# Key tile first in the opening, scalings on GpSimd, and another timetable for the attention steps of a decoder layer on eight cores

## The chip, the cores and the metric

One program runs on the 8 NeuronCores of one Trainium2 chip. Each core has a TensorE (PE), a VectorE (DVE), a ScalarE (ACT), a GpSimd (POOL), a SyncE (SP) that issues transfers, and 16 DMA engines. The metric is device time of the slowest core, in microseconds (us). The cores exchange nothing; each takes one of four sequences and one half of it.

## The reference

A decoder layer over `x` (4 x 4096 x 1024, float32) with a conditioning vector `c` per sequence. Cut to what matters here:

```python
mod = silu(c) @ w_ada + b_ada                      # (B, 6D): sh1, sc1, gt1, sh2, sc2, gt2
h   = rmsnorm(x, g_norm_mix) * (1 + sc1) + sh1
proj = h @ w_in + b_in                             # xin, bg, cg, q, k, v, o, gates, gate_c, gate_m
y_conv = bg * causal_dwconv(cg * xin, conv_mix_w)
hm  = mlstm_chunkwise(q, k, v, ig, fg)             # 128 tokens a chunk, a 128 x 256 state per head
z   = sigmoid(gate_c) * (y_conv @ w_proj_conv) + sigmoid(gate_m) * ((sigmoid(o) * headnorm(hm)) @ w_proj_mlstm)
x   = x + gt1 * (z @ w_out)
h   = rmsnorm(x, g_norm_ffn) * (1 + sc2) + sh2
a, g = split(h @ w_up)
x   = x + gt2 * ((silu(causal_dwconv(a)) * g) @ w_down)
out = rmsnorm(x, g_final)
```

The mLSTM carries a state through all 4096 tokens, so the core with the second half of a sequence needs the state that the first half leaves.

## The kernel before

**The prefix.** Each core first takes 2048 tokens (16 tiles of 128, the last one of 124) that stand before its own half. Of them it needs only the state: keys and gates for each tile, and one matrix. A tile n is loaded into a buffer of `xt` (10 buffers, queue of SP, `ask_x`), its sum of squares and root are made on ACT (L433, L436), the reciprocal and the scaling to bf16 on DVE (L442, L453), into `xnp[n]`. Four such tiles make a group. `tgroup` transposes a group on PE (32 matmuls against the identity, L484), and eight evacuations multiply by the gain `G1 = (1 + sc1) * g` and add the shift `sh1`: four on ACT (L488), four on DVE (L492). `kproj(c)` then makes the keys of a tile in 8 matmuls of 512 columns (L691), a DVE add of the bias (L693), and 8 small gate matmuls (L626).

**The opening's order.** POOL issues the weight transfers, which convert float32 to bf16, in the order in which they are first used: two tiles of `w_ada` for the scale (`ada_cols(2)`, `ada_cols(3)`), two for the shift (0 and 1), then the key tile of `w_in`; at most five are issued ahead until `allow_w` waits for an x tile and lifts the limit. Four x tiles are asked for at once, the next only when the third weight tile has landed. `ada_cols` is 32 matmuls of one column (L403). After the prefix come nine "front" tiles (the core's own first 4 + 1024 tokens), transposed in three groups into `hT`, then the gate matmuls of `stage_gates` and the projection of q, between whose four heads the steps of `gates_prefix` stand. Last comes the prefix state: 144 matmuls of 512 columns (L1348), which need every key tile scaled by the gate weights (L1337).

**The stages.** The core's own 2048 tokens are worked in two stages of 1024: projections (k, v, o), then a stretch in which the convolution branch's projections (x, c, b; `proj_blocks`, L508) run on PE while the mLSTM's chunk steps are put in between, then the merge, the output projection, and the FFN (up and down). Stage 0 has 9 chunks and blocks of 512, 258 and 258 columns, and 8 further blocks for modulation tiles (`unit_ada`); stage 1 has 8 chunks and blocks of 512.

**The table of the chunk steps.** `parts` (L1019) gives each step of chunk c a position in units of a chunk; position times `per` blocks says after how many projection blocks it is issued. The steps: `at_K` transposes the keys (PE L826, DVE L828), `at_A` makes the scores (PE L838, DVE L841 four times), `at_X` the outputs (PE L856 and L858 into banks 4 to 7, one ACT copy L860 of all four banks), `at_new` the new state (PE L867 into banks 4 to 7, DVE L869 four times), `at_old` the scaled bf16 state (ACT L847), `at_den`, `at_sq`, `at_f`, `at_hm` the head norm (DVE and ACT), `at_D` transposes back (PE L913, DVE L915 twice). During this stretch banks 4 to 7 are reserved for `at_X` and `at_new`; `at_K`, `at_A`, `at_D` and the projections take turns on banks 0 to 3 (`next_bank`). Every engine executes its own instructions in order.

**The down projection.** During the down projection of stage 0 (L1258), `during_down` loads, normalises (DVE L453) and transposes (PE L484) the x tiles of stage 1, one tile per output chunk; each tile's transfer is asked for in the same job that uses it.

## Time and profile before

| | us |
|---|---|
| median of 3 runs (lowest, highest) | 1375.95 (1372.84, 1376.09) |
| the profiled execution's own time | 1372.99 |
| its span on core 4, the slowest | 1371.7 |
| spans of the 8 cores | 1362.9 to 1371.7 |
| PE busy (share of the span) | 1263.1 (92%) |
| DVE, ACT, POOL busy | 697.5 (51%), 529.2 (39%), 76.5 (6%) |
| chain that ended last, PE's share | 83% |

All times below are microseconds from the start of the span on core 4. PEclk is the granted TensorE clock as a share of 2.4 GHz, 0.5 being 1.2 GHz. Idle time of an engine is named with what ended it ("<- DVE arena L453"). `arena` is one large buffer that holds most tiles, so a line number says more than its name.

### The profile page before, as it was taken

To read this page: it belongs to the slowest core of one execution; us is meant where nothing else is said; L and a number is where in the kernel's file an instruction comes from. 1 tells how busy PE (TensorE), PEld (TensorE's weight loads), DVE (VectorE), ACT (ScalarE), POOL (GpSimd) and SP (SyncE) were. 2 spreads that over 40 slices of the span, in tenths; PEclk is the share of its full clock that TensorE was granted. 3 is DMA by queue.
4 is the path that set the end of the run, shared out by engine and by line. 5 is a ranking of instruction groups with operands and counts; after the bars stand their busy time and mean duration, and the time that the engine had idled before them with its cause. 6 is when DMAs were issued, how large, how long until landed. Compare 5 with 4: busy or idle time off the path is not lost.

```text
span 1371.7 us, 21457 instructions; the slowest of 8 cores (1362.9 to 1371.7 us)
## 1 busy us (share of the span) xinstructions
PE 1263.1 (92%) x7662; PEld 690.8 (50%) x7662; DVE 697.5 (51%) x1268; ACT 529.2 (39%) x1013; POOL 76.5 (6%) x149
## 2 busy tenths in 40 slices
PE   0677999997899999999998999989999999999998
PEld 0354455665656665666654444444444444444443
DVE  0574332576843346555654423378732365556534
ACT  2464122654522225544433331465522245544202
POOL 1000000000000000000000000000000000100000
PEclk9997999999999999999999999999999999999999
DMA  9988024267493646343252782505346074441503
GB/s 174 233 194 136 1 39 75 50 107 124 85 189 60 106 91 131 69 81 63 46 111 85 175 154 54 101 1 93 84 101 112 13 152 93 74 81 32 108 0 123
DMA packets 35128, 130.38 MB, mean 95 GB/s; under 512 B 2764, under 2 KB 3020, under 8 KB 35024
## 3 DMA queue, kind: packets, MB, share of 16 engines
q0 software_dynamic: 24944, 93.74, 40.6%
q1 hardware_dynamic: 10080, 35.27, 7.8%
q8 instruction: 64, 1.05, 0.3%
q14 instruction: 40, 0.33, 0.1%
HBM read 214.34 MB, written 8.39 MB: 162 GB/s over the span
## 4 chain that ended last, share of the span: by engine, by line
PE 83%; DVE 6%; DMA 4%; ACT 3%; issue 3%; POOL 0%; DVEq 0%; ACTq 0%; SPq 0%; POOLq 0%
PE psum L508 54%; PE psum L1258 11%; PE psum L1113 4%; PE psum L793 4%; DMA wslot<-w_in 3%; PE psum L1348 2%; PE psum L691 2%; PE psum L484 1%; DVE C L869 1%; DVE arena L841 1%; ACT arena L860 1%; PE psum L867 1%; DMA arena<-bada_row 1%; ACT sqj L433 1%; PE psum L418 1%
## 5 line engine op out<-in xcount | busy, mean ns | idle before, releaser
L508 PE MATMUL psum<-arena,wslot 128*128 128x512 bf16 (+1 forms) x4640 | 830.7, 339 | 11.6 <-DVE arena L915 3.8
L508 PEld LDWEIGHTS psum<-arena,wslot 128*128 128x128 bf16 x4640 | 452.5, 98 | 372.0 <-issue 31.6
L1187 DVE SCALAR_TENSOR_TENSOR arena<-arena,pcol_t 128x1028 f32<-128x1028 f32 (+1 forms) x88 | 113.3, 1287 | 92.8 <-ACT arena L1184 88.2
L1258 PE MATMUL psum<-wslot,arena 128*128 128x512 bf16 x704 | 153.2, 380 | 1.5 <-ACT arena L488 1.5
L1258 PEld LDWEIGHTS psum<-wslot,arena 128*128 128x128 bf16 x704 | 68.8, 98 | 84.2 <-issue 2.2
L1069 ACT ACTIVATE arena<-psum,pcol_t 128x512 bf16<-128x512 f32 (+1 forms) x80 | 47.9, 603 | 162.2 <-PE psum L508 161.1
L433 ACT ACTIVATE sqj<-arena 128x1024 bf16<-128x1024 f32 (+1 forms) x49 | 51.6, 1054 | 137.6 <-DVE arena L1261 96.0
L1189 ACT ACTIVATE arena<-arena 128x1028 f32<-128x1028 f32 (+1 forms) x44 | 46.6, 1059 | 121.1 <-DVE arena L1187 121.1
L1073 DVE TENSOR_TENSOR arena<-psum,arena 128x512 f32<-128x512 f32 (+1 forms) x40 | 23.3, 585 | 73.4 <-PE psum L508 72.5
L1113 PE MATMUL psum<-wslot,arena 128*128 128x512 bf16 (+1 forms) x272 | 60.3, 379 | 0.2 <-DVE arena L492 0.2
L793 PE MATMUL psum<-wslot,arena 128*128 128x512 bf16 (+1 forms) x272 | 59.2, 379 | 0.0
L488 ACT ACTIVATE arena<-psum,modc,G 128x384 bf16<-128x384 f32 (+4 forms) x64 | 39.3, 670 | 50.3 <-PE psum L484 24.2
L1195 DVE TENSOR_TENSOR arena<-psum,arena 128x512 bf16<-128x512 f32 (+1 forms) x110 | 57.8, 575 | 0.0
L1077 DVE TENSOR_TENSOR arena<-psum,arena 128x512 bf16<-128x512 f32 (+1 forms) x40 | 23.3, 583 | 67.9 <-PE psum L508 67.9
L1172 ACT ACTIVATE arena<-psum 128x512 f32<-128x512 f32 (+1 forms) x110 | 51.8, 504 | 15.0 <-PE psum L508 14.0
L887 ACT ACTIVATE sqj<-arena,sml 128x256 bf16<-128x256 f32 (+1 forms) x68 | 33.7, 497 | 59.1 <-DVE sml L881 55.0
L126 POOL DMA_DIRECT2D wslot<-w_in x32 | 22.7, 710 | 601.7 <-PE psum L508 266.3
L1184 ACT ACTIVATE arena<-arena,pcol_t 128x1028 f32<-128x1028 f32 (+1 forms) x44 | 50.6, 1150 | 14.5 <-DVE arena L1178 11.4
L1261 DVE TENSOR_TENSOR arena<-psum,arena 128x512 f32<-128x512 f32 x32 | 22.1, 692 | 66.3 <-PE psum L1258 66.3
L796 DVE TENSOR_TENSOR arena<-psum,bvbc 128x512 bf16<-128x512 f32 (+1 forms) x34 | 23.6, 694 | 42.2 <-PE psum L793 42.2
L403 PE MATMUL psum<-scol,wslot 128*128 128x1 bf16 x256 | 7.7, 164 | 40.4 <-DMA wslot<-w_ada 38.5
L492 DVE TENSOR_SCALAR arena<-psum,G,modc 128x384 bf16<-128x384 f32 (+4 forms) x64 | 39.9, 671 | 6.8 <-PE psum L484 6.6
(176 smaller groups left out, 1084.8 us busy)
## 6 DMA issues: line engine op xcount, KB each, us to landing
wslot<-w_in POOLq DMA_DIRECT2D x32, 1024.0 KB, 12.2
arena<-xin SPq DMA_DIRECT2D x32, 512.0 KB, 16.1
wslot<-w_ada POOLq DMA_DIRECT2D x12, 1024.0 KB, 13.3
wslot<-w_up_a POOLq DMA_DIRECT2D x10, 1024.0 KB, 10.1
wslot<-w_up_g POOLq DMA_DIRECT2D x10, 1024.0 KB, 11.8
wslot<-w_down POOLq DMA_DIRECT2D x8, 1024.0 KB, 9.0
y<-arena SPq DMA_DIRECT2D x16, 512.0 KB, 2.7
xt<-xin SPq DMA_DIRECT2D x15, 512.0 KB, 5.2
```

Source lines behind the costliest of these rows:

```text
L433: S.op("act", lambda e: e.activation(out=sqj[0:p, :], in_=src, func=AF.Square, accum_out=ssq[0:p]), reads=r_src, writes=[r_sqj, r_ssq])
L492: S.op("dve", lambda e: e.tensor_scalar(out=dst[:, k, col0:col0 + n], in0=psum[:, b, 0:n], scalar1=G[:, k:k + 1], scalar2=modc[:, sh0 + k: ...
L508: S.op("pe", lambda e: e.matmul(psum[:, b, 0:n], lhsT=wv[:, k, wcol0:wcol0 + 128], rhs=src[:, k, t0:t0 + n], start=(k == 0), stop=(k == 7) ...
L793: S.op("pe", lambda e: e.matmul(psum[0:p, b, :], lhsT=hT[:, k, t0:t0 + p], rhs=wslot[si_v[half]][:, k, :], start=(k == 0), stop=(k == 7)), ...
L1069: S.op("act", lambda e: e.activation(out=sg[:, t0:t0 + n], in_=psum[:, b, 0:n], func=AF.Sigmoid, bias=pcol[:, PC_B + col:PC_B + col + 1]), ...
L1113: S.op("pe", lambda e: e.matmul(psum[0:p, b, :], lhsT=zT[:, k, t0:t0 + p], rhs=wslot[si_w[i]][:, k, :], start=(k == 0), stop=(k == 7)), re ...
L1172: S.op("act", lambda e: e.activation(out=a_s[:, 2 + t0:2 + t0 + n], in_=psum[:, b, 0:n], func=AF.Copy), reads=[r_bank[b]], writes=[r_a])
L1184: S.op("act", lambda e: e.activation(out=t3[:, T0:NT], in_=a_s[:, 2 + T0:2 + NT], func=AF.Identity, scale=pcol[:, cw + 2:cw + 3]), reads=[ ...
L1187: S.op("dve", lambda e: e.scalar_tensor_tensor(out=t3[:, T0:NT], in0=a_s[:, s_ + T0:s_ + NT], scalar=pcol[:, cw + s_:cw + s_ + 1], in1=t3[ ...
L1189: S.op("act", lambda e: e.activation(out=t3[:, T0:NT], in_=t3[:, T0:NT], func=AF.Silu), reads=[r_t], writes=[r_t])
L1195: S.op("dve", lambda e: e.tensor_tensor(out=act_t[j][:, t0:t0 + n], in0=psum[:, b, 0:n], in1=t3[:, t0:t0 + n], op=ALU.mult), reads=[r_bank ...
L1258: S.op("pe", lambda e: e.matmul(psum[:, b, :], lhsT=act_t[jj][:, t0:t0 + 128], rhs=wv[:, jj % 8, :], start=(jj == 0), stop=(jj == NFF - 1) ...
```

## The change

1. **Order of the opening.** The weight order becomes scale tiles, key tile, shift tiles. x tiles 4 to 7 are asked for when the key tile has landed (`sp_after(2)`), the rest when the second shift tile has (`sp_after(4)`). Groups 0 and 1 of the prefix are evacuated with the gain alone (`transp_plain`); keys 0 to 5 leave PSUM without a bias. `ada_cols(0)` and `ada_cols(1)` come behind `kproj(3)`. The shift's contribution to keys and gates is one row, made as 16 + 16 matmuls behind `kproj(5)` from a high and a low bf16 half of the shift broadcast over 128 columns, and added later: to keys 0 to 5 by three DVE adds behind `kproj(8)` to `kproj(10)`, to keys 6 and 7 in their evacuation, to the gates at the end.
2. **Scalings on GpSimd.** For the 16 prefix and 9 front tiles the multiplication by the reciprocal root runs on POOL. The norms are issued further ahead (`norm_upto`), with four more buffers (`xfr`) for front tiles. Evacuations of transposes in the opening go to ACT every fourth time, no longer every second.
3. **gates_prefix** gets two heads of the key projection of stage 0 as further cover.
4. **Chunk steps.** `at_K` is evacuated by four ACT instructions instead of one on DVE and uses bank 6, `at_A` bank 7, `at_D` banks 4 and 5. `at_new`, `at_old` and `at_D` are split in halves; the table of positions is another one.
5. **during_down** asks for each x tile one job ahead.

```diff
@@ opening
+        S.dma("pool", bkbc, brow_d[:, 0:512].partition_broadcast(128), writes=[r_bk])
         if plan is not None:
             pump_w()
-        S.dma("pool", bkbc, brow_d[:, 0:512].partition_broadcast(128), writes=[r_bk])
...
-            norm_to(xt[i][0:p, :], [r_xt[i]], dst[0:p, :], r_dst, p)
+            src = xt[i][0:p, :]
+            sd, r_sd = rms_root(src, [r_xt[i]], p)
+            rs, r_rs = recip(sd, r_sd, p)
+            S.op("pool", lambda e: e.tensor_scalar(out=dst[0:p, :], in0=src, scalar1=rs, scalar2=None, op0=ALU.mult),
+                 reads=[r_xt[i], r_rs], writes=[r_dst])
...
         ask_x(4)
-        ada_cols(2)
-        ada_cols(3)
-        ada_cols(0)
-        ask_x()
-        for c in range(4):
-            xprefix(c)
-        ada_cols(1)
+        sp_after(2)
+        ask_x(8)
+        sp_after(4)
+        ask_x()
+        norm_upto(4)
+        tiles0 = [(xnp[c], r_xnp[c], 128) for c in range(4)]
+        banks0 = [transp_mm(tiles0, k) for k in range(6)]
+        ada_cols(2)
+        ada_cols(3)
         gain(G1, r_G1, 8, PC_GMIX)
+        for k in range(6):
+            transp_plain(tiles0, hTp[0], r_hTp[0], k, banks0[k])
...
+        NB = 6
+        for c in range(NPF):
+            norm_upto((5, 6, 7, 8, 9, 10, 11, 12, 14, 16, 18, 20, 21, 22, 23, 24)[c])
+            if c == 9:
+                allow_w(6, r_xt[xbuf[15]])
+            if c == 3:
+                tiles1 = [(xnp[i], r_xnp[i], 128) for i in range(4, 8)]
+                for k in range(8):
+                    transp_plain(tiles1, hTp[1], r_hTp[1], k, transp_mm(tiles1, k))
+            if c in (7, 11):
+                tgroup(c // 4 + 1)
+            kproj(c)
+            if c == 3:
+                ada_cols(0)
+                ada_cols(1)
...
+            if c == NB - 1:
...
+                    S.op("pe", lambda e: e.matmul(psum[:, b, :], lhsT=shbc[:, i, :], rhs=wslot[si_k][:, i % 8, :], start=(i == 0), stop=(i == 15)),
...
@@ gates_prefix
-        interleave(gates_prefix(NPF), [(lambda h=h: proj(si_q, h * 128, hT, rd_h, tbs0, evq(h))) for h in range(4)])
+        interleave(gates_prefix(NPF), [(lambda h=h: proj(si_q, h * 128, hT, rd_h, tbs0, evq(h))) for h in range(4)]
+                   + [(lambda h=h: proj(si_k, h * 128, hT, rd_h, tbs0, evk(h))) for h in range(2)])
@@ chunk steps
-            parts = [(-0.7, at_K), (-0.7, at_A), (0.2, at_X), (0.3, at_new), (0.3, at_den), (0.45, lambda c: at_sq(c, lo)), (0.55, lambda c: at_sq(c, hi)),
-                     (0.65, at_f), (0.75, lambda c: at_hm(c, lo)), (0.85, lambda c: at_hm(c, hi)), (1.45, at_D)]
-            per = nblk / (nch + 0.6)
+            parts = [(-0.42, at_K), (-0.52, at_A), (0.05, at_X), (0.22, lambda c: at_new(c, lo)), (0.22, at_den), (0.3, lambda c: at_new(c, hi)),
+                     (0.35, lambda c: at_sq(c, lo)), (0.45, lambda c: at_sq(c, hi)), (0.6, at_f), (0.7, lambda c: at_hm(c, lo)), (0.8, lambda c: at_hm(c, hi)),
+                     (1.45, lambda c: at_D(c, (0,))), (1.53, lambda c: at_D(c, (1,)))]
+            per = nblk / (nch + 0.65)
+            todo = [((c + 0.2 + f) * per, i, fn, c) for c in range(nch) for i, (f, fn) in enumerate(parts)]
...
@@ during_down
+                        if c + 1 < len(chunks):
+                            asked.append(load_x(chunks[c + 1][2], chunks[c + 1][1]))
```

Where the order moves, it is shown engine by engine. PE's queue in the opening, from the first key projections on, before (L691 is a key projection, L484 a transpose, L403 a modulation tile):

```order
2 L691 MATMUL psum<-wslot,arena 128x512 x8
3 L626 MATMUL psum<-wgate,arena 128x8 x8
4 L691 MATMUL psum<-wslot,arena 128x512 x8
5 L626 MATMUL psum<-wgate,arena 128x8 x8
6 L691 MATMUL psum<-wslot,arena 128x512 x8
7 L626 MATMUL psum<-wgate,arena 128x8 x8
8 L484 MATMUL psum<-identb,arena 128x128 x32
9 L691 MATMUL psum<-wslot,arena 128x512 x8
```

and now (L739 is the key projection, L488 the transpose, L409 a modulation tile, L775 and L778 the shift's row):

```order
7 L739 MATMUL psum<-wslot,arena 128x512 x8
8 L647 MATMUL psum<-wgate,arena 128x8 x8
9 L488 MATMUL psum<-identb,arena 128x128 x32
10 L739 MATMUL psum<-wslot,arena 128x512 x8
11 L647 MATMUL psum<-wgate,arena 128x8 x8
12 L409 MATMUL psum<-scol,wslot 128x1 x64
13 L739 MATMUL psum<-wslot,arena 128x512 x8
14 L647 MATMUL psum<-wgate,arena 128x8 x8
15 L739 MATMUL psum<-wslot,arena 128x512 x8
16 L647 MATMUL psum<-wgate,arena 128x8 x8
17 L775 MATMUL psum<-wslot,arena 128x512 x16
18 L778 MATMUL psum<-wgate,arena 128x8 x16
```

The transposes of group 1 stand ahead of the fourth key projection, as they did; two modulation tiles and the shift's row now stand behind them.

POOL's queue in the opening now, from the scaling of x tile 14 on (`d_sp10` is the semaphore of the transfer of x tile 21, `s_dve` the reciprocal):

```order
30 L681 TENSOR_SCALAR arena<-arena,stat 128x1024 [waits d_sp3,s_dve]
31 L681 TENSOR_SCALAR arena<-arena,stat 124x1024 [waits d_sp4,s_dve]
32 L126 DMA wslot5<-w_in 128x2x2048 [waits d_sp10]
33 L681 TENSOR_SCALAR xnb0<-xt0,stat 4x1024 [waits d_sp5,s_dve]
34 L681 TENSOR_SCALAR xnb1<-xt1,stat 128x1024 [waits d_sp6,s_dve]
35 L681 TENSOR_SCALAR xnb2<-arena,stat 128x1024 [waits d_sp7,s_dve]
```

Before, this queue held only transfers here; now the scalings of the nine front tiles stand behind a transfer that waits for x tile 21.

PE's queue in the chunk steps of stage 1, the third chunk before (L826 `at_K`, L838 `at_A`, L867 `at_new`, L913 `at_D`, L508 projection blocks, 8 matmuls each):

```order
555 L858 MATMUL psum<-Cb,arena 128x257
556 L826 MATMUL psum<-identb,arena 128x128 x4
557 L838 MATMUL psum<-arena 128x128 x4
558 L867 MATMUL psum<-arena 128x257 x4
559 L508 MATMUL psum<-arena,wslot 128x512 x8
560 L913 MATMUL psum<-identb,xnb 128x128 x8
561 L508 MATMUL psum<-arena,wslot 128x512 x32
```

and now (L900 `at_K`, L911 `at_A`, L938 `at_new`, L984 `at_D`, L529 projection blocks):

```order
613 L929 MATMUL psum<-Cb,arena 128x257
614 L529 MATMUL psum<-arena,wslot 128x512 x8
615 L938 MATMUL psum<-arena 128x257 x4
616 L529 MATMUL psum<-arena,wslot 128x512 x8
617 L984 MATMUL psum<-identb,xnb 128x128 x4
618 L911 MATMUL psum<-arena 128x128 x4
619 L529 MATMUL psum<-arena,wslot 128x512 x8
620 L984 MATMUL psum<-identb,xnb 128x128 x4
621 L900 MATMUL psum<-identb,arena 128x128 x4
622 L529 MATMUL psum<-arena,wslot 128x512 x24
```

A projection block now stands between the outputs (`at_X`) and `at_new`, and the steps that stood together stand apart.

## Rows read from the trace of the kernel before

**Rows 1.** Stretches: PE, PEld, DVE, ACT, POOL busy, PEclk, DMA share, GB/s
```profile
94.00:134.00 40.00, 27.93 (x251) 19.10 (x251) 18.63 (x57) 22.34 (x45) 3.63 (x5) 0.77 0.85 140
...
248.00:392.00 144.00, 124.56 (x990) 81.77 (x990) 102.83 (x242) 72.49 (x188) 10.18 (x14) 0.95 0.59 98
...
880.00:984.00 104.00, 94.37 (x555) 49.51 (x553) 81.34 (x178) 60.77 (x150) 3.52 (x5) 0.98 0.24 43
```
**Rows 2.** PE's timeline: start, length, instructions [idle before <- what ended it]
```profile
32.55 0.99 PE L403 MATMUL psum<-scol,wslot 128*128 128x1 bf16 x32 [5.55 <-DMA wslot<-w_ada]
...
42.34 3.57 PE L484 MATMUL psum<-identb,arena 128*128 128x128 bf16 x32
50.66 3.57 PE L691 MATMUL psum<-wslot,arena 128*128 128x512 bf16 x8 [4.75 <-DMA wslot<-w_in]
...
59.98 1.78 PE L484 MATMUL psum<-identb,arena 128*128 128x128 bf16 x29 [1.51 <-DVE arena L453]
61.59 1.89 PE L691 MATMUL psum<-wslot,arena 128*128 128x512 bf16 x8
...
112.46 5.24 PE L508 MATMUL psum<-arena,wslot 128*128 128x512 bf16 x24
```
**Rows 3.** ACT's timeline, the square of x tile 7
```profile
56.36 1.06 ACT L433 ACTIVATE sqj<-arena 128x1024 bf16<-128x1024 f32 x1 [2.73 <-DMA arena<-xin]
```
**Rows 4.** POOL's groups by form, 0 to 20: busy, mean ns of one
```profile
L374 POOL TENSOR_SCALAR_AFFINE_SELECT identf<-identf 128x128 f32<-128x128 f32 x1 | 0.3, 289 | 0.1
L161 POOL MEMSET const-float32-0.0<- 128x1 f32 x1 | 0.1, 93 | 0.5 <-issue 0.5
```
**Rows 5.** DVE's timeline in the opening
```profile
81.40 0.75 DVE L453 TENSOR_SCALAR arena<-arena,stat 124x1024 bf16<-124x1024 f32 x1
82.85 2.95 DVE L492 TENSOR_SCALAR arena<-psum,G,modc 128x508 bf16<-128x508 f32 x4 [0.70 <-PE psum L484]
85.94 0.69 DVE L693 TENSOR_TENSOR arena<-psum,arena 128x512 bf16<-128x512 f32 x1
...
95.47 1.91 DVE L492 TENSOR_SCALAR arena<-psum,G,modc 128x260 bf16<-128x260 f32 x4
...
108.45 2.60 DVE L492 TENSOR_SCALAR arena<-psum,G,modc 128x384 bf16<-128x384 f32 x4 [0.84 <-PE psum L484]
132.94 9.72 DVE L1337 TENSOR_TENSOR arena<-arena,gm_wGp 128x512 bf16<-128x512 bf16 x16 [0.45 <-ACT gm_wGp L587]
```
**Rows 6.** Issue of x tile 17 (71.2) to landing; then of 22 (87.9)
```profile
xt<-xin SPq DMA_DIRECT2D x1, 512.0 KB, 9.8
xt<-xin SPq DMA_DIRECT2D x1, 512.0 KB, 4.0
```
**Rows 7.** PE's timeline behind the projection of q
```profile
131.76 0.40 PE L583 MATMUL psum<-gr_mp,onesf 1*128 1x64 f32 x2 [2.34 <-DVE gr_mp L576]
133.89 0.58 PE L1348 MATMUL psum<-arena,onesb 128*128 128x512 bf16 x1 [1.73 <-DVE arena L1337]
...
139.93 0.38 PE L1348 MATMUL psum<-arena,onesb 128*128 128x512 bf16 x1
...
141.01 0.38 PE L1348 MATMUL psum<-arena,onesb 128*128 128x512 bf16 x1
```
**Rows 8.** PE's timeline, transposes within the down projection
```profile
723.61 2.50 PE L484 MATMUL psum<-identb,xnb 128*128 128x128 bf16 x22 [3.96 <-DVE xnb L453]
...
742.59 1.47 PE L484 MATMUL psum<-identb,xnb 128*128 128x128 bf16 x22 [1.76 <-DVE xnb L453]
```
**Rows 9.** PE's waits, 225 to 400: in total, times, longest
```profile
PE psum L508 <- DVE arena L915: 3.6, 1, 3.6
```
**Rows 10.** PE's waits, 880 to 1010
```profile
PE psum L867 <- ACT arena L860: 6.9, 6, 1.9
```
**Rows 11.** PE's timeline, stage 0: 32 matmuls of 258 columns, twice
```profile
314.77 4.53 PE L508 MATMUL psum<-arena,wslot 128*128 128x258 bf16 x32
...
335.32 7.30 PE L508 MATMUL psum<-arena,wslot 128*128 128x258 bf16 x32 [3.61 <-DVE arena L915]
```

More of the change, by code:

```diff
@@ L277, in _build @@
         bkbc = at("E", 3 * 2048, [128, 512], BF16)
+        bksh = at("E", 7168, [128, 512], BF16)
+        shbc = at("F", 16384, [128, 16, 128], BF16)
+        gsh_t = sb("gsh", [128, 8])
+        gsh = gsh_t[:]
+        shhl = sb("shhl", [128, 16], BF16)
+        xfr = [at("E", 8192 + i * 2048, [128, D], BF16) for i in range(4)]
         r_wslot = RL("wslot", NSLOT)
@@ L692, in kproj @@
                      reads=[r_src[k], r_wslot[si_k]], writes=[r_bank[b]], inc=(k == 7))
-            S.op("dve", lambda e: e.tensor_tensor(out=kwp[0:p, c, :], in0=psum[0:p, b, :], in1=bkbc[0:p, :], op=ALU.add),
-                 reads=[r_bank[b], r_bk], writes=[r_kwp[c]])
-            gate_mm(src, r_src, c, o, p, GBK)
-        front_tiles = []
-        def front_norm(f):
-            j = state["xnb"]
-            state["xnb"] = (j + 1) % 4
-            norm_x(NPF + f, xnb[j], r_xnb[j])
-            front_tiles.append((xnb[j], r_xnb[j], xseq[NPF + f][1]))
@@ L705, in _build @@
-        tgroup(0)
-        for g in range(4):
-            for i in range(4):
-                if g < 3:
-                    xprefix(g * 4 + 4 + i)
-                elif i < 3:
-                    front_norm(i)
-                if g < 3 and i == 3:
-                    tgroup(g + 1)
-                kproj(g * 4 + i)
-            if g == 1:
-                allow_w(6, r_xt[xbuf[13]])
+            if c < NB:
+                S.op("dve", lambda e: e.tensor_copy(out=kwp[0:p, c, :], in_=psum[0:p, b, :]), reads=[r_bank[b]], writes=[r_kwp[c]])
+            else:
+                bt, r_bt = (bksh, r_bksh) if c < 8 else (bkbc, r_bk)
+                S.op("dve", lambda e: e.tensor_tensor(out=kwp[0:p, c, :], in0=psum[0:p, b, :], in1=bt[0:p, :], op=ALU.add),
+                     reads=[r_bank[b], r_bt], writes=[r_kwp[c]])
@@ L717, in _build @@
         gate_evac(graw, r_graw, GBK, 0, NPF - 1, 128)
+        S.op("dve", lambda e: e.tensor_tensor(out=graw[:, 0:8, :], in0=graw[:, 0:8, :], in1=gsh.rearrange("p (o g) -> p o g", o=1).to_broadcast([128, 8, 8]),
+                                              op=ALU.add), reads=[r_graw, r_gsh], writes=[r_graw])
         gate_evac(graw, r_graw, GBK, NPF - 1, NPF, PLAST)
@@ L861, in at_X, with at_new @@
                      reads=r_bank[XB:XB + 4], writes=[r_Xs[0]], own=True)
-            def at_new(c):
+            def at_new(c, hh):
                 p = chunks[c][1]
-                for h in range(4):
+                for h in hh:
                     pb = XB + h
@@ L904, in at_hm, with at_D @@
                          reads=[r_Xs[0], r_f4[j]], writes=[r_hmb[jh]])
-            def at_D(c):
+            def at_D(c, halves):
                 j = c % 4
                 t0, p, _ = chunks[c]
-                for half in range(2):
-                    b = next_bank()
+                for half in halves:
+                    b = XB + half
                     for kk in range(4):
@@ L1285, in _build @@
         for g in range(3):
[L1286 to L1291 removed]
+            tiles = front_tiles[g * 3:g * 3 + 3]
+            transp(tiles, hT, LAY[0][0][g * 3][0], r_h0[g], G1, r_G1, SH1, 4)
+            norm_upto(NPF + 9)
         allow_w(1 << 30, r_xt[xbuf[NPF + 8]])
@@ L1302, in during_down @@
             seq, late, held = [], [], []
+            asked = [load_x(chunks[0][2], chunks[0][1])]
             def end():
```

110 lines of the change are left out of this document (74 added, 36 removed).

## The prediction, written before the result was known

> **What bounds the kernel now.** I read the chain of waits first (PE holds 83% of it), then the busy times by stretch, then PE's own timeline in the stretches where it isn't full. PE is 92% busy over the span, so a step pays only where PE stands still or runs at the lower clock, and there are four such places.
>
> First the opening. PE meets the key tile at 50.66, having waited for it [rows 2], then works through the prefix to 94, and reaches the projection of q at 112.46. From 94 to 134 it is busy for 27.9 of 40 us at a granted clock of 0.77 [rows 1]. Second, the gap behind q: it waits 2.34 and 1.73 us for the gates, and the first 15 state matmuls, three groups of five, run at 1.2 GHz [rows 7]. Third, waits for a normalised x tile in the down projection [rows 8]. Fourth, the chunk steps: PE idles 144 - 124.6 = 19.4 us from 248 to 392 and 104 - 94.4 = 9.6 us from 880 to 984, with mean clocks of 0.95 and 0.98 [rows 1].
>
> **Opening: what decides is x tile 7, not the key tile.** The third weight tile landed at 32.55 [rows 2]. Now it is the key tile, with a small bias transfer ahead; I put it at 33.8. Keys 0 to 2 can be made at once, some 17 us earlier. But PE's order then asks for the transposes of group 1 ahead of key 3, as it did before, and they need x tile 7. That tile was asked for when the third weight tile had landed, and came at 56.36, 23.8 us later, beside two weight tiles [rows 3]. The same two transfers (now the shift tiles) share the engines with x tiles 4 to 7 again, without the bias transfer. I take 22 us: 56. Before, 3.6 us lay between that landing and PE's transposes at 59.98 [rows 2, 3]; scaling on POOL is longer than on DVE (0.75 [rows 5]), DVE's queue is emptier: 59.5. So the early key tile wins 0.5 us at this point.
>
> POOL's price for a scaling of 1024 columns no row shows. Its select over 128 columns took 289 ns, an empty memset 93 [rows 4]: 8 x 0.196 + 0.09 = 1.66 us above, DVE's 0.75 below. I take 1.3, nearer to POOL's own row.
>
> The Trainium skill (GPSIMD Engine Reference, 3.1 Elementwise) has 1.03 cycles an element for such bodies at 1.2 GHz, an estimate of 0.88 us and a dispatch; by it, four scalings on the path below would be 1 to 1.6 us cheaper in all. No row here shows it.
>
> From 59.5 PE has more to do than before. It stood still for 20 us, so the 32 transposes cost what those at 42.34 did, 3.6 [rows 2]: 63.1. Key 3 at 1.9 [rows 2]: 65.0. Two modulation tiles at 1.0 [rows 2], formerly in a wait: 67.0. Keys 4, 5: 70.8. The shift's row, 16 matmuls at 1.89 / 8 each, 3.8 [rows 2]: 74.6. Key 6: 76.5. Then PE waits for tile 11: DVE's evacuation 0.7, reciprocal, POOL 1.3: 78.8. Transposes 1.8, key 7: 82.5. Before it ended at 74.2 by the same steps: 61.59, keys 3 to 6 at 1.9, a wait of 1.5, transposes 1.6, key 7 [rows 2].
>
> The x stream decides the rest. DVE has six evacuations of 0.74 per group now [rows 5], until 83.5, then key 7's and the reciprocals of 12 and 13 at 84.5; behind key 8 and the first add (two tiles at 0.61 [rows 5]) come those of 14 and 15 at 86.9. POOL ends tile 15 at 89.7. That frees the buffer for x tile 21, which lands 4.0 later, 93.7 [rows 6]. POOL waits just for it (the lifted limit of weight transfers stands ahead of tile 16's scaling), issues, and scales tile 16 at 95.7. Only then is tile 22 asked for, beside a weight tile: 9.8 us in the like case, 4.0 without [rows 6]; I take 8, 103.7, and tile 23 at 105.7. DVE holds their reciprocals ahead of the evacuations of keys 14 and 15 and of all front groups: square 1.1, root, reciprocal, evacuation: 108.8. Front groups: 6 x 0.48 + 12 x 0.63 = 10.4 [rows 5]: 119.2. Last gate matmuls: q starts at 120 against 112.46 [rows 2], **7 us later**. By 4.0 for tiles 22 and 23 it is 3; by 9.8, and POOL at 1.66, it is 11. If the x stream never holds DVE, PE's own work gives 82.5 + 8 x 1.9 + 1.8, then 10.4 and 0.8: 110.7, 2 us earlier.
>
> **Gap behind q.** Two heads of k (moved, not added) cover the scan of the gates: the wait of 2.34 goes, 1.73 stays, since it hangs on the state's first scaled key tile. The state matmuls follow dense work. From 133.89 to 139.93 three groups of five took 6.0 us; at the pitch of the next group, 139.93 to 141.01, they take 3.2 [rows 7]. **-5.1**. At worst the clock part stays: -2.3.
>
> **Down projection.** With the tile loaded a job ahead the wait of 3.96 becomes what the second group showed, 1.76, DVE's own evacuation and scaling; the transposes behind it go from 2.50 to 1.47 at the full clock [rows 8]. **-3.2**, between 0 and -4.
>
> **Chunk steps.** Two mechanisms. PE waited 6.9 us in six places for the ACT copy before `at_new` [rows 10]; a block of 1.9 us now stands between in seven of eight chunks of stage 1. And `at_K`, `at_A`, `at_D` took four of the turns on banks 0 to 3 in each chunk; now projections have them alone, so that they tolerate more backlog on DVE. The longest wait, 3.6 us for `at_D`'s evacuation [rows 9], was such a backlog; the 32 matmuls behind it took 7.30 instead of 4.53 [rows 11]. What can be won: 19.4 + 9.6 idle, and by the mean clocks 0.05 x 144 + 0.02 x 104 = 9.3, together 38. Against it: `at_A` now waits for bank 7, which `at_new`'s last DVE update frees, often one block earlier; four ACT instructions replace one DVE; the burst of convolution instructions on DVE is as long as before. DVE is 71% and 78% busy here [rows 1], so backlogs remain. I take a third of it, **-13**, and keep +5 and -30 as ends.
>
> **Sum.** 7 - 5.1 - 3.2 - 13 = -14.3 against the profiled execution's own 1372.99: 1358.7. That execution lies 3 us under the median of the runs, 1375.95, so for the median 1361.6; I say 1361.
>
> **The rivals.**
> 1. The opening pays as it was meant to (the x stream runs ahead, tile 7 comes sooner). For it: an x tile alone lands 4.0 us after its issue [rows 6], so the stream can catch up. Against it: PE asks for tile 7 at the same place as before, and POOL stands still for tile 21. 2 us earlier instead of 7 later: 1352.
> 2. The chunk steps give most of their waits back: -30 in place of -13: 1344. For it: 6.9 of the 9.6 us in stage 1 are one kind of wait. Against: the bursts on DVE.
> 3. Slower. Bank 7 takes the place of the waits removed: `at_A` stands one block behind `at_new` and needs its four DVE updates, with key and convolution work in DVE's queue. If that costs 1 us a chunk beyond what other waits give back, 17 chunks make +10 at most; from about +4 on, with the opening at 7 to 10, the sum is above zero: 7 + 8 - 8.3 = +6.7, 1382. For it: DVE ended the longest wait of stage 0 [rows 9]. Against: `at_A`'s result is needed only a chunk later.
> 4. POOL is held up while DVE reads two operands from SBUF. Three adds of 1.2 us [rows 5] stand beside the scalings of tiles 12 to 17; each could shift the x stream by as much, 3.6 in all: 1365. The Trainium skill (GPSIMD Engine Reference, 8. Key points) says that POOL shares its SBUF interfaces with such DVE instructions. No row here shows both engines at it.
>
> **How the numbers follow.** Forecast 0.58, rival 1 0.14, rival 2 0.10, rival 3 0.11, rival 4 0.07. Differences under 0.3% (4 us) can't be told from none. The forecast's own range is 1350 to 1371, as the opening (3 to 11) and the chunk steps (-5 to -22) go. Taking in rival 2 nearly, and the near half of rival 3, 1343 to 1377 leaves out 2 in 10 at most. Faster by over 0.3% (under 1371.8): all of 1, 2 and most of 4 and the forecast, 0.84; same 0.07; slower (over 1380) 0.09.
>
> **What would show it.** In the profile after: the first key projection near 34 and a gap on PE from 40 to 59, ended by POOL; POOL idle before the transfer at 94, and the projection of q at 115 to 123 (right), near 111 (rival 1). Nothing over 2 us between the last projection of k and the state's first matmul, and those at the full clock. In the down projection no wait for `xnb` over 2 us. In the chunk steps waits of `at_new` for the copy under 2 us in all in stage 1; waits of `at_A` for DVE over 8 us in all would be rival 3. I am wrong if q starts before 112, or if PE's idle time in the chunk steps falls by more than 20 or doesn't fall.

## The result: 1% slower, and the profile after

| | before | after |
|---|---|---|
| median of 5 runs (lowest, highest), us | 1373.95 (1372.42, 1376.09) | 1388.75 (1387.37, 1604.44) |
| ratio | | 1.0101, 95% interval 1.0086 to 1.0117 |
| its span, slowest core | 1371.7 (core 4) | 1385.9 (core 7) |
| POOL busy | 76.5 | 147.8 |

I had said 1361, "faster" with a chance of 0.84. It is slower by 14.1 us (1388.07 against 1373.95), outside my range. (In some executions of any kernel the cores of one die or of both show a lower clock for part of the time and the time is longer; the table's medians hold them, while the ratios and all times from here on are of the others.)

Where the time went can be read by comparing when each stage's first matmul starts, median of the eight cores. The numbers are differences to the kernel before, in us: what a stage lost (+) or won (-).

| stretch | predicted | after |
|---|---|---|
| opening, up to the projection of q | +7 | +25.4 |
| from q to the projection of v | -5.1 | -4.1 |
| chunk steps of stage 0 | | -11.3 |
| behind them, up to the down projection | | +3.5 |
| chunk steps of stage 1 | -13 for all three | +1.4 |
| down projection of stage 0, with the x tiles | -3.2 | -0.8 |
| sum (with 0.2 elsewhere) | -14.3 | +14.4 |

The opening alone turns the sign. Its rows in the profile after, PE's timeline (start, length, engine, line, operation, idle time before it and what ended it), answer to [rows 2]; L739 is the key projection, L488 the transpose:

```profile
34.36 3.57 PE L739 MATMUL psum<-wslot,arena 128*128 128x512 bf16 x8 [4.05 <-DMA wslot<-w_in]
...
50.07 0.27 PE L488 MATMUL psum<-identb,arena 128*128 128x128 bf16 x1 [7.64 <-POOL arena L681]
...
60.66 3.25 PE L488 MATMUL psum<-identb,arena 128*128 128x128 bf16 x29 [2.55 <-POOL arena L681]
63.70 3.15 PE L739 MATMUL psum<-wslot,arena 128*128 128x512 bf16 x8
...
84.20 3.25 PE L488 MATMUL psum<-identb,arena 128*128 128x128 bf16 x29 [2.60 <-POOL arena L681]
...
103.43 3.23 PE L488 MATMUL psum<-identb,arena 124*128 124x124 bf16 x29 [2.55 <-POOL arena L681]
...
125.13 2.35 PE L488 MATMUL psum<-identb,xnb 4*128 4x4 bf16 x16 [6.08 <-DVE graw L652]
...
135.09 0.27 PE L488 MATMUL psum<-identb,xnb 128*128 128x128 bf16 x1 [2.55 <-POOL xnb L681]
...
140.01 5.96 PE L529 MATMUL psum<-arena,wslot 128*128 128x512 bf16 x24
```

The key tile comes at 34.36 and the gap behind the first three keys ends at 60.66, both near the forecast (34 and 59.5). The second is partly luck: the square of x tile 7 starts on ACT at 54.36, so the tile had landed 1.6 us or more before my 56, and POOL's longer scalings of tiles 6 and 7 took that up. Then it parts from the forecast: groups 2 and 3 and the front groups wait for POOL each time. The distance between two waits, 2.55 + 0.27 = 2.82 us, is the duration of one scaling. POOL's groups by form, up to 160 us (busy, mean ns of one), and its timeline:

```profile
L681 POOL TENSOR_SCALAR arena<-arena,stat 128x1024 bf16<-128x1024 f32 x13 | 36.8, 2841 | 45.6 <-DVE stat L448 45.6
L681 POOL TENSOR_SCALAR xnb<-xt,stat 4x1024 bf16<-4x1024 f32 x1 | 2.8, 2833 | 0.0
```
```profile
91.96 11.32 POOL L681 TENSOR_SCALAR arena<-arena,stat 128x1024 bf16<-128x1024 f32 x4 [7.91 <-DVE stat L448]
108.74 0.77 POOL L126 DMA_DIRECT2D wslot<-w_in  x1 [5.45 <-DMA arena<-xin]
109.55 5.66 POOL L681 TENSOR_SCALAR xnb<-xt,stat 4x1024 bf16<-4x1024 f32 x2
...
132.12 2.83 POOL L681 TENSOR_SCALAR xnb<-arena,stat 128x1024 bf16<-128x1024 f32 x1
```

A scaling costs 2.84 us, twice my 1.3 and above my upper bound of 1.66. One on 4 partitions takes as long as one on 128. POOL's stand for x tile 21 is there, 5.45 us, and so is DVE's hold by late reciprocals (PE's wait of 6.08). So POOL costs in two ways. In the prefix it isn't full: from 84.20 to 103.43 it stands still for 7.91 us, until DVE has made the reciprocals behind the last key's evacuation, and then its 11.32 us stand in series with PE's work. For the front tiles it is full: nine scalings follow each other from 109.55 to 134.95, and PE's last group of transposes starts at 135.09.

### The profile page after: what moved, and what is told of

It is laid out like the page before. It is cut to its first block, busy times and chain, and to the rows that moved or that the text cites. A ratio compares the mean times of both kernels' runs of the same rounds, so it can differ in the third digit from the quotient of the medians.

```text
span 1385.9 us, 21577 instructions; the slowest of 8 cores (1378.0 to 1385.9 us)
## 1 busy us (share of the span) xinstructions
PE 1268.0 (91%) x7694; PEld 697.1 (50%) x7694; DVE 682.4 (49%) x1248; ACT 537.6 (39%) x1068; POOL 147.8 (11%) x174
## 4 chain that ended last, share of the span: by engine, by line
PE 82%; DMA 5%; DVE 4%; issue 3%; ACT 3%; POOL 2%; DVEq 0%; ACTq 0%; POOLq 0%; SPq 0%
PE psum L529 54%; PE psum L1330 11%; PE psum L1185 4%; PE psum L865 4%; DMA wslot<-w_ada 3%; PE psum L1421 2%; PE psum L488 2%; POOL arena L681 1%; PE psum L739 1%; DMA arena<-bada_row 1%; PE psum L938 1%; ACT xnb L974 1%; ACT sqj L439 1%; DMA xt<-xin 1%; ACT arena L931 1%
## 5 line engine op out<-in xcount | busy, mean ns | idle before, releaser
L529 PE MATMUL psum<-arena,wslot 128*128 128x512 bf16 (+1 forms) x4640 | 829.7, 339 | 8.3 <-DVE arena L986 5.7
L529 PEld LDWEIGHTS psum<-arena,wslot 128*128 128x128 bf16 x4640 | 452.2, 98 | 358.2 <-issue 19.3
L488 PE MATMUL psum<-identb,arena 128*128 128x128 bf16 (+1 forms) x160 | 21.2, 305 | 55.5 <-POOL arena L681 54.0
L1244 ACT ACTIVATE arena<-psum 128x512 f32<-128x512 f32 (+1 forms) x110 | 51.4, 505 | 14.4 <-PE psum L529 12.2
L1256 ACT ACTIVATE arena<-arena,pcol_t 128x1028 f32<-128x1028 f32 (+1 forms) x44 | 50.6, 1150 | 14.1 <-DVE arena L1250 11.0
L448 DVE RECIPROCAL stat<-stat 128x1 f32<-128x1 f32 (+1 forms) x66 | 10.3, 159 | 84.0 <-ACT stat L442 83.9
L488 PEld LDWEIGHTS psum<-identb,arena 128*128 128x128 bf16 (+1 forms) x160 | 17.0, 142 | 57.5 <-issue 57.5
```

What stands on the lines that cost most here:

```text
L488: S.op("pe", lambda e: e.matmul(psum[:, b, c:c + p], lhsT=a[0:p, k * 128:(k + 1) * 128], rhs=identb[0:p, 0:p], start=True, stop=True), rea ...
L529: S.op("pe", lambda e: e.matmul(psum[:, b, 0:n], lhsT=wv[:, k, wcol0:wcol0 + 128], rhs=src[:, k, t0:t0 + n], start=(k == 0), stop=(k == 7) ...
L1244: S.op("act", lambda e: e.activation(out=a_s[:, 2 + t0:2 + t0 + n], in_=psum[:, b, 0:n], func=AF.Copy), reads=[r_bank[b]], writes=[r_a])
L1256: S.op("act", lambda e: e.activation(out=t3[:, T0:NT], in_=a_s[:, 2 + T0:2 + NT], func=AF.Identity, scale=pcol[:, cw + 2:cw + 3]), reads=[ ...
```

## Experiments on the opening

Times are medians unless single ones are given; ratios are to the kernel before on the same chip, where it took 1372 to 1374. The stage times are those of the profiled executions, medians of the eight cores.

**One word back: the scalings on DVE.**
```diff
-            S.op("pool", lambda e: e.tensor_scalar(out=dst[0:p, :], in0=src, scalar1=rs, ...
+            S.op("dve", lambda e: e.tensor_scalar(out=dst[0:p, :], in0=src, scalar1=rs, ...
```


> The changed kernel with one word changed: the 25 scalings of x tiles run on DVE again, all else as changed. Theory A (POOL's price: the trace after has 2.84 us for a scaling, against my 1.3 and DVE's 0.75, and PE waits for POOL 57.7 us in 16 waits): the projection of q starts at 116 to 119 in place of 138 to 140 and the time falls by about 20 us, to about 1368. Theory B (the new order itself costs: 5.7 us more work on PE, the reciprocals of late x tiles in DVE's queue ahead of evacuations): q starts at 128 or later and the time is 1376 or more.

1367.72, ratio 0.9966 (0.9952 to 0.998). q starts at 119.6, 6.8 us later than before; after, it was 25.4. Theory A holds: POOL's price, against DVE's, is 18.6 of the 25.4, and the new order costs the 7 I gave it. DVE's row for the same instruction:

```profile
L681 DVE TENSOR_SCALAR arena<-arena,stat 128x1024 bf16<-128x1024 f32 x13 | 9.8, 753 | 1.4
```

**The same price in the old order.** The kernel before, only with its 25 scalings on POOL.
```diff
-            norm_to(xt[i][0:p, :], [r_xt[i]], dst[0:p, :], r_dst, p)
+            sd, r_sd = rms_root(src, [r_xt[i]], p)
+            rs, r_rs = recip(sd, r_sd, p)
+            S.op("pool", lambda e: e.tensor_scalar(out=dst[0:p, :], in0=src, scalar1=rs, ...
```


> The kernel before with the 25 scalings on POOL and nothing else changed. If the price of POOL alone explains the opening (Theory A), some 20 us are lost here too, about 1394, with q at 130 or later. By the rows, a group of four scalings takes POOL 11.4 us and PE has 9.3 us of work on a group, so the rival (price and order together make the loss) expects POOL's excess of 2 us a group, +2 to +6 us in all: 1376 to 1380, q at 114 to 119.

1413.85, ratio 1.0312 (1.0292 to 1.0332): 41 us lost, more than either side expected. By the stage times 27.3 are lost up to q, and 15 more until the chunk steps of stage 0, where PE doesn't wait at all; of those below. Up to q the cause is in the order: here a reciprocal is issued just ahead of its key projection, behind the evacuation of the projection ahead of it (L697), so POOL starts a group only when the last one's keys are being made. Its POOL timeline, then PE's:

```profile
86.50 11.30 POOL L660 TENSOR_SCALAR arena<-arena,stat 128x1024 bf16<-128x1024 f32 x4 [5.33 <-DVE stat L442]
```
```profile
80.60 3.13 PE L484 MATMUL psum<-identb,arena 128*128 128x128 bf16 x29 [2.55 <-POOL arena L660]
...
97.95 3.22 PE L484 MATMUL psum<-identb,arena 124*128 124x124 bf16 x29 [2.56 <-POOL arena L660]
```

A group takes 17.35 us (97.95 - 80.60): 11.3 of POOL and, in series with it, transposes, evacuation and first key. My row arithmetic (11.4 beside 9.3) had put them side by side. Issuing the norms further ahead (`norm_upto`) doesn't undo this in the prefix: after, the like group takes 19.23 us (103.43 - 84.20). Over the whole opening the price costs less there, 18.6 for 27.3.

Of the 15 us behind q, 12 stand at a lower granted clock. Stretches of this kernel (length, busy times, with PE's first, then granted clock, DMA share, GB/s), and of the kernel before; the first two of each are the same work:

```profile
164.00:226.00 62.00, 61.84 (x282) 30.77 (x283) 20.21 (x63) 13.34 (x26) 0.71 (x1) 0.80 0.13 20
226.00:290.00 64.00, 64.00 (x341) 33.85 (x340) 19.07 (x29) 13.71 (x26) 2.39 (x3) 0.93 0.43 66
170.00:250.00 80.00, 80.00 (x362) 38.52 (x361) 22.44 (x67) 13.89 (x29) 0.71 (x1) 0.81 0.11 17
```
```profile
134.00:188.00 54.00, 53.50 (x287) 28.23 (x287) 19.97 (x64) 13.26 (x26) 0.70 (x1) 0.95 0.08 15
188.00:248.00 60.00, 60.00 (x344) 32.93 (x343) 18.86 (x29) 14.27 (x27) 2.12 (x3) 1.00 0.47 73
140.00:220.00 80.00, 79.50 (x423) 40.42 (x422) 26.78 (x74) 13.82 (x29) 1.41 (x2) 1.00 0.11 17
```
PE is full in both, and the same work takes 8 + 4 = 12 us more here. From 170 to 250 the granted clock was 0.81, neither of the two levels that the kernels before and after show, on all eight cores alike. Whether this kernel brings that level about isn't shown. Its mean clock is as low in all four executions (0.951 to 0.960 on every core). But the same 0.81 stands on two cores of another kernel's profile, whose other six cores do the same work without it: with the earlier head norm below, core 6 has it from 720 to 875, and core 0 has 1.00 there. So of the 41 us only the 27.3 up to q speak of POOL's price, and of these some 2 may be the clock (an estimate: five keys from 89 on at 2.30 us in place of 1.93).

**POOL's law.** After, each scaling in two instructions.
```diff
+            m = 512 if n < NPF else 256
+            for lo_, hi_ in ((0, m), (m, D)):
+                S.op("pool", lambda e: e.tensor_scalar(out=dst[0:p, lo_:hi_], in0=src[:, lo_:hi_], ...
```


> The changed kernel, each POOL scaling in two instructions: 512 + 512 columns for the prefix, 256 + 768 for the front. If POOL's price is one of columns (2.77 ns each, no fixed part to speak of): 1.42 and 0.71 and 2.13 us, and the time stays at 1389. If there is a large fixed part (the one on 4 partitions took as long as one on 128): about the same for all sizes, and 1400 or more.

```profile
L683 POOL TENSOR_SCALAR xnb<-arena,stat 128x256 bf16<-128x256 f32 x3 | 2.7, 913 | 0.0
L683 POOL TENSOR_SCALAR arena<-xt,stat 128x512 bf16<-128x512 f32 x8 | 12.4, 1561 | 3.8 <-DVE stat L448 3.8
L683 POOL TENSOR_SCALAR xnb<-arena,stat 128x768 bf16<-128x768 f32 x3 | 6.6, 2193 | 0.0
```
256, 512, 768 and 1024 columns take 0.91, 1.56 (1.61 in a part of the prefix), 2.19 and 2.84: (2.84 - 0.91) / 768 = 2.5 ns a column and 0.27 fixed. Nearly the first theory for the price; the fixed part is larger than it had. Its one execution gave 1408.3, with cores 4 and 5 at a mean granted clock of 0.95 against 0.97 on the others, so that time decides nothing; by the stage times q starts 4 us later than after.

**x tiles ahead of the key tile.** The version with scalings on DVE, and
```diff
-        ask_x(4)
-        sp_after(2)
-        ask_x(8)
+        ask_x(8)
+        sp_after(2)
```


> The changed kernel with its scalings on DVE (1368.1) and the x tiles 4 to 7 asked for at once with tiles 0 to 3, ahead of the wait for the key tile. There PE stands from 40 to 57 for x tile 7. Theory A (the tiles come late since they are asked for behind the key tile and share the engines with two shift tiles): four tiles of 4 us each ahead of the key tile put it at about 41 to 45, key 3 at about 50 in place of 60.7, and the front of q 5 to 9 us earlier: 1360 to 1364. Rival (the total of bytes to the last x tile sets q, whatever their order): q within 2 us of 119.6, 1366 to 1369.

Three executions took 1359.19 to 1362.01, ratio 0.9906 (0.9888 to 0.9923), against 0.9966 without. Theory A holds. The rows are read from the last version below, which has the same opening:

```profile
41.58 2.87 PE L738 MATMUL psum<-wslot,arena 128*128 128x512 bf16 x7 [7.00 <-ACT stat L442]
...
50.18 1.78 PE L488 MATMUL psum<-identb,arena 128*128 128x128 bf16 x29 [1.50 <-DVE arena L681]
52.01 1.67 PE L738 MATMUL psum<-wslot,arena 128*128 128x512 bf16 x7
```
Key 3 starts at 52.0, in place of 60.7 with the scalings on DVE alone and 63.7 after, though the first key starts 7 us later than after (41.58 for 34.36); q starts at 109.7, 3 us ahead of the kernel before. (The profile names ACT at the wait of 7.00. But the key projection reads nothing that this ACT line writes, and the key tile's transfer, issued at 4.18, took 36.8 us to land.) By this the early key tile had taken the DMA engines from the x tiles that PE needed next.

## Experiments on the rest

**The rest without the opening.** Parts 3 to 5 of the change on the kernel before. Its diff is that of the change without the opening.

> The changed kernel with the opening (order, scalings, shift row) of the kernel before; the cover of the gates, the down projection's transfers and the chunk steps stay as changed. If the stages' differences add (opening +25.4 of a total of +14.4), the time is about 11 us under the kernel before: 1363. The rival, that the later stages gained only because the opening ended late (DMA transfers ready, clock), expects less than half of it: 1369 or more.

1361.78, ratio 0.9917 (0.9892 to 0.9941): 10.6 us under the kernel before. The stages add up: q to v -4.4, stage 0 -10.8. It is the base of the kernels below, called the base (the expectations below have it at 1362.2).

**The chunk steps alone** (part 4 on the kernel before).

> The kernel before with the new chunk steps alone (banks, halves, ACT evacuation of the keys, table of positions). By the stage times of the two traces: -11.3 in stage 0, +3.5 just behind it, +1.4 in stage 1, so -6.4 us, about 1367.5. My prediction had -13 (1361); a rival that the gain was in fact a gain of the other parts has 0 (1374).

1365.02, ratio 0.9952 (0.9938 to 0.9967): -6.6, as the stage times had it, half of my -13.

**Banks back.**
```diff
-                b = XB + 2
+                b = next_bank()
...
-                b = XB + 3
+                b = next_bank()
...
-                    b = XB + half
+                    b = next_bank()
```


> The changed kernel with the old opening (1362.2), and at_K, at_A and at_D again taking turns with the projections on banks 0 to 3; halves, ACT evacuation of the keys and the new table stay. In it PE waits 6.7 us in stage 0 for bank 7 (at_A for the state updates on DVE). If banks 0 to 3 for the projections alone made the gain of stage 0 (my second mechanism), stage 0 loses 4 or more: 1366 or more. If the table and the relief of DVE made it, the waits for bank 7 go and others stay as they are: 1356 to 1361.

Two executions took 1373.81 and 1374.49 (no interval), 12.4 over the base. Stage 0 loses 10.7 us and stage 1 6.0 against it; 4.2 come back just behind stage 0. PE's waits in stage 0 (total, times, longest), base first:

```profile
PE psum L839 <- DVE C L868: 6.7, 5, 2.9
PE psum L866 <- ACT arena L859: 3.0, 3, 1.9
```
```profile
PE psum L828 <- DVE arena L914: 5.9, 2, 3.1
PE psum L508 <- DVE sml L895: 3.5, 1, 3.5
PE psum L912 <- DVE gt2bc L420: 3.0, 1, 3.0
```
With the old banks projections (L508), `at_K` (L828) and `at_D` (L912) wait for DVE. With the new ones the only wait for DVE of size is `at_A`'s for bank 7 (L839), 6.7: rival 3's mechanism exists, and costs less than it replaces (12.4 us for these three rows alone).

**The keys back on DVE.** One DVE instruction in place of four on ACT in `at_K`.

> The changed kernel with the old opening (1362.2), and the keys of at_K evacuated by one DVE instruction again, bank 6 and the table staying. If the relief of DVE makes the gain of stage 0 (DVE was the bound of its bursts), most of the 11 us go: about 1370. If the banks of their own make it, the time stays within 2 us: 1361 to 1364. ACT's queue gets 8 x 0.7 us shorter in stage 1, where PE waits 8.0 us for the copy of at_X on ACT, so stage 1 may win 1 to 2.

1366.1, ratio 0.9949 (0.9931 to 0.9967), 4.3 over the base. Stage 0 +0.8, stage 1 +2.0: neither expectation for the total met (it lies between), but the stages side with the banks. ACT's shorter queue won nothing in stage 1; PE's wait for the copy grew from the base's 8.0:

```profile
PE psum L867 <- ACT arena L860: 9.5, 4, 3.7
```

**Why stage 1 wins nothing.** There the banks are worth 6.0 and the keys 2.0, and yet it takes 1.4 to 2.0 more than before. The wait that I had expected under 2 us is in the profile after 7.6:

```profile
PE psum L938 <- ACT arena L931: 7.6, 4, 3.1
```
The base shows its chain. DVE, then ACT, then PE:

```profile
920.92 2.67 DVE L977 SCALAR_TENSOR_TENSOR arena<-arena,pcol_t 128x1024 f32<-128x1024 f32 x2
923.51 0.17 DVE L895 RECIPROCAL sml<-sml 128x4 f32<-128x4 f32 x1
```
```profile
924.04 0.91 ACT L902 ACTIVATE xnb<-arena,sml 128x256 bf16<-128x256 f32 x2 [5.70 <-DVE sml L896]
...
926.79 1.01 ACT L859 ACTIVATE arena<-psum 128x1028 f32<-128x1028 f32 x1
```
```profile
927.95 1.02 PE L866 MATMUL psum<-arena 128*128 128x257 bf16 x4 [3.06 <-ACT arena L859]
```
The reciprocal of `at_f` stands behind a burst of convolution on DVE; ACT waits 5.70 for it with `at_hm` (L902), and the copy (L859) for the next chunk's `at_new` stands behind that. The block that PE has between `at_X` and `at_new` can't help, since the copy starts late. Two kernels test this. First the distances of the head norm as before:

```diff
-                     (0.35, lambda c: at_sq(c, lo)), (0.45, lambda c: at_sq(c, hi)), (0.6, at_f), (0.7, lambda c: at_hm(c, lo)), (0.8, lambda c: at_hm(c, hi)),
+                     (0.3, lambda c: at_sq(c, lo)), (0.4, lambda c: at_sq(c, hi)), (0.5, at_f), (0.6, lambda c: at_hm(c, lo)), (0.7, lambda c: at_hm(c, hi)),
```


> The changed kernel with the old opening (1362.2), and the head norm's steps at the distances from at_X that they had before (at_sq at 0.3 and 0.4, at_f 0.5, at_hm 0.6 and 0.7, each 0.05 to 0.1 earlier than changed). Banks and ACT's keys are worth 6.0 and 2.0 us in stage 1 by the two kernels that undo them, and yet stage 1 takes 1 to 2 us more than before, so something in the table costs some 10 there. If it is the later head norm (at_hm close ahead of the next copy on ACT), stage 1 wins 3 to 6 us: 1356 to 1359. If it is something else (at_K and at_A 0.2 to 0.3 later, at_new in halves), under 1.5 us: 1361 or more.

Two executions took 1353.43 and 1354.03, 8 us under the base (ratio 0.9828, 0.9724 to 0.9933; the interval is wide since two of the eight executions of the kernel before took 1388 and 1391). Stage 1 is 6.7 us shorter than the base's, and the wait for the copy falls from 8.0 to 2.7 (core 0). The table's later head norm is the cause. Then two buffers:

```diff
-        Xs = [at("F", 14560, [128, 4, 257])]
+        Xs = [at("F", 14560 + i * 2064, [128, 4, 258], BF16) for i in range(2)]
...
-                     ... (0.6, at_f), (0.7, lambda c: at_hm(c, lo)), (0.8, lambda c: at_hm(c, hi)),
+                     ... (0.9, at_f), (1.1, lambda c: at_hm(c, lo)), (1.2, lambda c: at_hm(c, hi)),
```


> The changed kernel with the old opening (1362.2), and two buffers (in bf16) for the copy of at_X in place of one, with the head norm's last step (at_hm) moved behind the next chunk's copy and at_f to 0.9. In stage 1 PE waits 8.0 us for the copy; by the rows the copy stands in ACT's queue behind at_hm, that waits for DVE's reciprocal (at_f) behind a burst of convolution. If that chain is the cause, the waits of at_new for the copy fall under 2 us, stage 1 takes 5 to 7 us less and stage 0 up to 2: 1354 to 1357. Rival (ACT itself is too full, or the wait only moves to at_D): under 2 us of gain, 1360 or more.

1357.51, ratio 0.9881 (0.9862 to 0.99). Stage 1 -6.5, the wait 1.3 us; stage 0 -0.2, so the hoped-for 2 there didn't come.

**The down projection.** There the trace after reads like that before, to 0.01 us, though each tile is asked for a job earlier [rows 8]:

```profile
736.28 2.51 PE L488 MATMUL psum<-identb,xnb 128*128 128x128 bf16 x22 [3.96 <-DVE xnb L459]
...
756.60 1.46 PE L488 MATMUL psum<-identb,xnb 128*128 128x128 bf16 x22 [1.76 <-DVE xnb L459]
```
What the wait is made of stood in DVE's timeline of the kernel before:

```profile
719.65 0.69 DVE L1261 TENSOR_TENSOR arena<-psum,arena 128x512 f32<-128x512 f32 x1 [0.93 <-PE psum L1258]
720.25 2.28 DVE L1208 TENSOR_TENSOR wslot<-wslot,gt2bc 128x4096 bf16<-128x4096 bf16 x1
722.72 0.75 DVE L453 TENSOR_SCALAR xnb<-xt,stat 128x1024 bf16<-128x1024 f32 x1
```
PE issues the transposes as soon as an output chunk ends, and DVE then has 0.69 + 2.28 + 1.0 of work ahead of them. On the base, the transposes one job later:

```diff
-                    seq.append([end] + late + [one])
-                    late = []
-                late = [lambda g=g, tiles=tiles: transp(...)]
+                    seq.append([end] + late.pop(0) + [one])
+                    late.append([])
+                late[1] = [lambda g=g, tiles=tiles: transp(...)]
```


> The changed kernel with the old opening (1362.2), and in the down projection of stage 0 the transposes of a group issued one job (one output chunk, 4.7 us) later. There PE waits 3.97 and 1.76 us, in the kernel with the transfers ahead exactly as before. By DVE's rows the wait is its evacuation (0.69), a multiplication of a weight tile (2.28, in the first only), reciprocal and scaling (1.0). If so, both waits go and the transposes run at the full clock: stage 4 to 7 us shorter, 1355 to 1358. Rival (PE waits as long elsewhere, for DVE's evacuations of the outputs or the gates): under 2 us.

1352.15, 9.6 under the base (ratio 0.9801, 0.9671 to 0.9931). Both waits are gone but for 0.3 us and the stage is 7.7 us shorter, 1.7 of which come back in the next:

```profile
708.99 1.50 PE L484 MATMUL psum<-identb,xnb 128*128 128x128 bf16 x24
```

**A failed one: the rows of biases apart.** Just behind stage 0 the base waits 4.05 us for DVE (after: 5.71), which waits for the second row of biases.
```diff
-                units += [...] + ([unit_ada(j + 3)] if first else []) + [unit_c(j)]
+                units += [...] + ([unit_ada({6: 10, 7: 9}.get(j, j + 3))] if first else []) + [unit_c(j)]
```


> The changed kernel with the old opening (1362.2), and the two modulation tiles that need a row of biases no longer next to each other (10 in place of 9 and 9 in place of 10). Just behind stage 0 PE waits some 5 us for DVE, which waits for the second row's transfer: it can only be issued when the first has been used, and shares the engines with seven x tiles. If the transfer is the cause, that wait goes and 3 to 5 us are won: 1357.5 to 1359.5. Rival: the wait is then for DVE's own backlog and stays, 1361 or more.

Two executions took 1361.47 and 1361.89, ratio 0.9913 (0.9891 to 0.9934): no gain. The transfer was the cause of a part: DVE no longer waits for it (2.18 us in the base) and PE's wait for DVE falls from 4.05 to 1.78, but PE then waits for a weight tile:

```profile
374.96 10.62 PE L508 MATMUL psum<-arena,wslot 128*128 128x512 bf16 x72 [1.78 <-DVE arena L914]
389.68 10.53 PE L508 MATMUL psum<-arena,wslot 128*128 128x512 bf16 x53 [4.10 <-DMA wslot<-w_proj_mlstm]
```
Whether that tile would have been late in the base too is left open.

**Together.** After, with scalings on DVE, `ask_x(8)` at once, two copies and the later transposes.

> The changed kernel with scalings on DVE, x tiles 4 to 7 asked for at once, two copies of at_X and the later transposes in the down projection. If the gains add to the 1360.7 of the first two: 6.5 and 6 less, 1347 to 1350. If the opening's gain was of the fast runs' scatter: 1355 or more.

> The best kernel so far a second time, for a tighter interval: 1339 to 1344, a ratio of 0.975 to 0.979 to the kernel before.

1341.44 and, in the second series, 1342.43 (ratio 0.9744, 0.9684 to 0.9805, with the same two executions of the kernel before in it). By the medians of that series, 1372.94 and 1342.43, it is some 30 us faster than the kernel before, and 46 faster than the change as it was. I had expected 1347 to 1350. By the stage times the opening is 10 us shorter than with scalings on DVE alone, and the down projection's stage 8.2 shorter than the base's, where I had counted 7.4 and 6. Last, `at_K` at -0.52 and `at_A` at -0.35 on top of it:

> The best kernel so far (1341.7: scalings on DVE, x tiles asked for at once, two copies, later transposes) with at_K ahead of at_A and at_A at -0.35 in place of -0.52. PE waits 6.8 us in stage 0 and 2.7 in stage 1 for bank 7, which the last state update on DVE frees. If one more block between the update and at_A takes that wait away, 4 to 7 us: 1335 to 1338. If DVE's backlog sets the time of the update, whatever PE does, or at_X then waits for at_A's scores: 1340 or more.

1349.94, ratio 0.98 (0.9732 to 0.9869): 7 slower than without. In stage 0 the wait of 6.6 for the state updates, at `at_A` and bank 7, becomes one of 4.7 at `at_K` (L899) and bank 6, since `at_K` now stands first. And `at_X` (L926) now waits: the profile names a reciprocal (L966), but the scores (L913), which it reads, end just ahead of it, 0.15 us before PE starts at 274.26, behind a burst of convolution:

```profile
PE psum L926 <- DVE sml L966: 4.8, 3, 2.1
PE psum L899 <- DVE C L939: 4.7, 4, 2.6
```

## Why the prediction was wrong, step by step

- **POOL's price: the step that failed.** I bounded it by "a select over 128 columns took 289 ns, an empty memset 93", extrapolated to 1.66 at most, and took 1.3; it is 2.84. The error of the bound is that another operation's slope (1.53 ns a column, from a short tile) stood for this one's 2.5. Put into my own steps, 2.84 moves tile 15 from 89.7 to 99 (1.5 us each at tiles 7 and 11, then 4 x 2.84 in series) and tile 21 to 103; and a term appears that at 1.3 I had left out, the nine front scalings on POOL, 9 x 2.84 = 25.6: 128.6, and q, which starts 5.1 behind the last of them in the trace after, at 134, 21 us later than before. That is an estimate; 25.4 was measured. So the price failed, and with it the picture of an opening that the x stream decides: it is decided by scalings that PE waits for. The version with DVE's 0.75 gave +6.8. The Trainium skill (GPSIMD Engine Reference, 3.1 Elementwise), which has 1.03 cycles an element for short bodies, an estimate of 0.88 us, is further off still: at its 1.2 GHz the measured 2.5 ns are 3.0 cycles.
- **Opening, order.** Right in what POOL doesn't decide: x tile 7, not the key tile, ends the gap (60.66 for 59.5, by an earlier landing and a dearer scaling; 57.17 with the scalings on DVE), the shift row 3.6 for 3.8, POOL's stand for tile 21, DVE held by late reciprocals. By the version on DVE: 6.8 for 7.
- **Gap behind q.** Right: -4.1 (-4.4 in the base) for -5.1. The 2.34 went, the 1.73 stayed [rows 7], and the first state matmuls run at the full clock:

```profile
166.75 0.38 PE L1421 MATMUL psum<-arena,onesb 128*128 128x512 bf16 x1 [1.73 <-DVE arena L1410]
166.97 1.02 PE L1421 MATMUL psum<-arena 128*128 128x512 bf16 x4
```
- **Down projection.** Wrong: nothing at the two waits for -3.2. I took the wait of 3.96 for a late transfer, because the second was 1.76. Both are DVE's work; the difference is a weight multiplication of 2.28 between them. A look at DVE's timeline in that window would have shown it.
- **Chunk steps.** -6.4 for -13. The mechanism of the banks was right and is worth more than the total (10.7 and 6.0). The other, a block between `at_X` and `at_new`, was wrong: I read who ended the wait (the copy) and not what the copy waited for. The table's later head norm cost some 7 us in stage 1 and turned its gain to a loss.
- **Rivals.** Rival 3 (bank 7) has its wait, 7.1 us in stage 0 and 2.3 in stage 1 after, in all 9.4 and so over the 8 that I had named as its sign, but not its price: the banks win on balance, and the sign was a poor one. The slower result came by another way, POOL, which I had as a cost of 1.3 and not as a rival that could bound the opening. Rival 4 is answered by the trace after. DVE's three adds stand beside the scalings of tiles 12 to 14, and none of the 14 scalings in this group took over 2.865 us, the shortest 2.832. What gives way is DVE, once: two adds took 0.68 us as they do with POOL idle, and one 1.30 (on every core). Why only that one is open.

```profile
L681 POOL TENSOR_SCALAR arena<-arena,stat x14: 2832/2842/2865, 16.3 to 123.7; 128x1024 bf16<-128x1024 f32 x13, 124x1024 bf16<-124x1024 f32 x1
```
```profile
93.21 0.68 DVE L784 TENSOR_TENSOR arena<-arena 128x1024 bf16<-128x1024 bf16 x1
...
95.13 1.30 DVE L784 TENSOR_TENSOR arena<-arena 128x1024 bf16<-128x1024 bf16 x1
```
